# Paged decode attention: keys turned by VectorE in 32x32 blocks, block-diagonal queries

## What is computed

```python
def stick_breaking_weights(z, mask):
    log_keep = jnp.where(mask, jax.nn.log_sigmoid(-z), 0.0)
    remain = lax.cumsum(log_keep, axis=z.ndim - 1, reverse=True)
    return jnp.exp(jnp.where(mask, z + remain, -jnp.inf))

def sb_decode(q, k_new, v_new, k_past, v_past, bias):
    z_past = jnp.einsum('bqhd,bkhd->bhqk', q, k_past)
    z_new = jnp.einsum('bqhd,bkhd->bhqk', q, k_new)
    z = jnp.concatenate([z_past, z_new], axis=-1) * scale + bias[None, :, None, None]
    a = stick_breaking_weights(z, mask)          # mask: all of the past, causal in the new tokens
    return (jnp.einsum('bhqk,bkhd->bqhd', a[..., :P], v_past)
            + jnp.einsum('bhqk,bkhd->bqhd', a[..., P:], v_new))
```

## Time and profile before

| | us |
|---|---|
| timed runs, median of 3 | 1451.14 |
| lowest and highest | 1446.97, 1455.94 |
| span of the profiled execution | 1442.7 |
| PE busy in it | 1288.7 (89%) |
| VectorE busy | 400.6 (28%) |
| ScalarE busy | 353.6 (25%) |
| DMA, mean over the span | 274 GB/s |

### The profile page before, as it was taken

How to read it: one execution, slowest core, us unless ns; L and a number is a source line. 1 busy time by engine, 2 the same in 40 slices (tenths; PEclk the granted TensorE clock), 3 DMA queues, 4 the chain that set the end, 5 groups by cost and what they waited for, 6 DMA issues and landing times.

```text
span 1442.7 us, 22498 instructions
## 1 busy us (share of the span) xinstructions
PE 1288.7 (89%) x8892; PEld 778.3 (54%) x8892; DVE 400.6 (28%) x745; ACT 353.6 (25%) x575; POOL 87.3 (6%) x146
## 2 busy tenths in 40 slices
PE   7999999989999999878999999789987888788782
PEld 4787555756777666546888865533332333333231
DVE  2012565634544445431101123511111001101103
ACT  2122344444554445642000011200000000000000
POOL 3000000020000002000000000011101000100000
PEclk9999999999999989999999999889999889999887
DMA  6113301068999989999911150299999999999985
GB/s 237 59 59 117 111 1 61 27 182 302 386 375 381 379 303 386 385 386 348 392 35 37 59 235 31 88 367 427 424 425 426 425 426 426 426 425 426 427 367 198
DMA packets 119641, 395.96 MB, mean 274 GB/s; under 512 B 17075, under 2 KB 25284, under 8 KB 107250
## 3 DMA queue, kind: packets, MB, share of 16 engines
q1 hardware_dynamic: 109506, 380.41, 67.7%
q0 software_dynamic: 5984, 11.18, 2.2%
q10 hardware_dynamic: 4048, 2.93, 0.6%
HBM read 386.06 MB, written 16.27 MB: 279 GB/s over the span
## 4 chain that ended last, share of the span: by engine, by line
PE 79%; issue 7%; SPq 7%; DMA 4%; DVE 2%; ACT 1%; POOLq 0%; DVEq 0%
PE ps L1180 17%; PE ps L1002 8%; PE ps L694 8%; PE ps L1203 7%; PE ps L824 5%; PE ps L697 5%; PE ps L1005 4%; PE ps L1067 4%; SPq L411 3%; PE ps L858 3%; SPq L399 3%; PE ps L835 3%; DMA arena<-in_w_in 2%; DMA arena<-in_cache_k 1%; PE ps L1191 1%
## 5 line engine op out<-in xcount | busy, mean ns | idle before, releaser
L1180 PE MATMUL ps<-arena 128*64 128x512 f32 x512 | 253.8, 654 | 69.3 <-issue 67.8
L1181 PE MATMUL ps<-arena 128*64 128x512 f32 x512 | 254.3, 655 | 0.0
L1180 PEld LDWEIGHTS ps<-arena 128*64 128x64 f32 x512 | 74.2, 151 | 215.0 <-issue 212.9
L824 PE MATMUL ps<-ident,arena 128*128 128x128 f32 x1024 | 142.8, 283 | 25.4 <-DMA arena<-in_cache_k 24.9
L824 PEld LDWEIGHTS ps<-ident,arena 128*128 128x128 f32 x1024 | 112.3, 143 | 91.3 <-issue 59.3
L1410 ACT ACTIVATE arena<-ps 128x512 f32<-128x512 f32 x192 | 108.2, 596 | 162.7 <-PE ps L824 162.5
L1002 PE MATMUL ps<-mixers,arena 128*128 128x272 f32 x512 | 121.6, 399 | 4.9 <-DMA arena<-in_w_in 4.9
L694 PE MATMUL ps<-mixers,arena 128*128 128x272 f32 x512 | 119.3, 393 | 0.0
L1002 PEld LDWEIGHTS ps<-mixers,arena 128*128 128x128 f32 x512 | 98.8, 194 | 25.9 <-DMA arena<-in_w_in 5.1
L694 PEld LDWEIGHTS ps<-mixers,arena 128*128 128x128 f32 x512 | 96.7, 190 | 20.3 <-issue 0.4
L1821 DVE COPY arena<-ps 128x512 f32<-128x512 f32 x64 | 44.2, 691 | 163.9 <-PE ps L824 163.9
(11 more groups left out here) (343 smaller groups left out, 1393.2 us busy)
## 6 DMA issues: line engine op xcount, KB each, us to landing
arena<-in_cache_k SPq DMA_DIRECT2D x256, 256.0 KB, 5.6
arena<-in_w_gate_exp SPq DMA_DIRECT2D x32, 2048.0 KB, 32.4
arena<-in_w_up_exp SPq DMA_DIRECT2D x32, 2048.0 KB, 36.9
arena<-in_cache_v SPq DMA_DIRECT2D x252, 256.0 KB, 5.9
arena<-in_w_down_exp SPq DMA_DIRECT2D x22, 2048.0 KB, 37.6
mixers<-in_w_down_exp SPq DMA_DIRECT2D x10, 2048.0 KB, 37.7
arena<-in_w_in SPq DMA_DIRECT2D x7, 2048.0 KB, 9.4
arena<-in_w_in SPq DMA_DIRECT2D x8, 1024.0 KB, 15.6
```

The lines of the kernel that those rows point to most:

```text
L824: last = turn(ps[:, turned_at(n, j), P * c:P * c + P], keys_of(n)[:, j, P * c:P * c + P], ident[:, :])
L1180: mm(ps[0:BLK, 1 + u, :], own, wgv[w][:, k, :], start=k == 0, stop=k == KD - 1)
L1181: last = mm(ps[BLK:P, 1 + u, :], own, wuv[w][:, k, :], start=k == 0, stop=k == KD - 1)
```

## The change

**Keys.** PE no longer turns pages. VectorE turns a unit's four pages in one instruction, in blocks of 32x32 (`keys_turned`): input 128 x 2048 floats, output 128 x 2048, SBUF to SBUF. After it, partition 32g + k holds dimension k of a 32-wide slice of a head, for the tokens 32g to 32g + 31 of each page. The scores are therefore products with block-diagonal queries: 16 products of 128 columns in place of 4 of 512, with the queries of one sequence set out by four quarters of the tokens (`query_rows`, `query_blocks`, `in_g`).

**Sets.** A set is now four units of one sequence. A row of the score tile is a head pair, a quarter g of every page, and a query; the sum over the past needs what the other three quarters add. Two small products per set (`other_losses`) with two constant matrices, made by GpSimd in place of masks no longer used, bring it, and VectorE subtracts it in one more 128x512 instruction (`remains`).

**Values.** The turned weights have token 32g + r of page j at partition 4r + j. So the values are loaded in that order: page j goes to the 32 partitions j, j + 4, ..., and each of them receives four rows of the page, 2 KB each and 32 rows apart. The products have 8 rows instead of 32. A unit's four value loads stay 256 KB each.

```diff
@@ loads @@
-                b, g = PER_SET * (m // NGRP) + s, m % NGRP
-                first_page = b * NPAGES + NPAGES - GP * (g + 1)
+                b, later = m // SETS_OF, SETS_OF - 1 - m % SETS_OF
+                first_page = b * NPAGES + GP * (PER_SET * later + s)
             def key_loads(n):
                 if n >= 3:
-                    sp.wait_ge(S("page_turned"), GP * (n - 2))
+                    sp.wait_ge(S("keys_turned"), n - 2)
             def value_loads(n):
                 for j, page in enumerate(numbers):
-                    sp.dma_start(values_of(n)[:, j, :], a["cache_v"][0, bass.ds(page, 1)].rearrange("a s h d -> (a s) (h d)")
-                                 ).then_inc(S(values_signal(n)[0]), 16)
+                    sp.dma_start(values_of(n)[j::GP], a["cache_v"][0, bass.ds(page, 1)].rearrange(
+                        "a (g s) h d -> (a s) g (h d)", g=4)).then_inc(S(values_signal(n)[0]), 16)
@@ PE @@
-            def turn_pages(n, pair):
...
+                pe.wait_ge(S("keys_turned"), n + 1)
-                for c in range(CT):
-                    last = mm(ps[32 * c:32 * c + 32, ZB, :], qblk_of(m // NGRP, s, c), d_kt[:, n % 2, c, :],
-                              start=s == 0, stop=s == PER_SET - 1)
+                for x in range(4):
+                    for c in range(CT):
+                        last = mm(ps[32 * c:32 * c + 32, ZB, P * s:P * s + P], wq[:, m // SETS_OF % 2, 4 * c + x, :],
+                                  d_kt[:, n % 2, 4 * c + x, :], start=x == 0, stop=x == 3)
+            def other_losses(m):
+                pe.wait_ge(S("set_ends"), m + 1)
+                mm(ps[:, bank, 0:16], neg_lt, own[:, 0:16], start=True, stop=False)
+                mm(ps[:, bank, 0:16], tri_ge, own[:, 1:17], start=False, stop=True).then_inc(S("other_losses"), 1)
@@ unit_values @@
-                        last = mm(ps[32 * c:32 * c + 32, VB, P * s:P * s + P], d_at[:, m % 2, j, 32 * c:32 * c + 32],
-                                  values_of(n)[:, j, P * c:P * c + P], start=m % NGRP == 0 and s == 0 and j == 0,
+                        own = d_at[:, m % 2, s, 32 * c + 8 * g:32 * c + 8 * g + 8]
+                        last = mm(ps[32 * c:32 * c + 8, VB, at:at + P], own,
+                                  values_of(n)[:, g, P * c:P * c + P], start=n % SEQ_UNITS == 0 and g == 0,
@@ VectorE @@
-                    v.tensor_copy(d_kt[:, n % 2, :, P * j:P * j + P], each(ps[:, turned_at(n, j), :], CT)).then_inc(S("kT_dve"), 1)
+            def keys_turned(n):
+                dve.wait_ge(S(f"cache_k_{n % 3}"), (n // 3 + 1) * 16 * GP)
+                if n >= 2:
+                    dve.wait_ge(S("unit_scores"), n - 1)
+                out = d_kt[:, n % 2].rearrange("p b (j k) -> p j b k", j=GP)
+                v.transpose(out, keys_of(n).rearrange("p j (b k) -> p j b k", k=32)).then_inc(S("keys_turned"), 1)
+            def remains(m):
+                dve.wait_ge(S("other_losses"), m + 1)
+                v.tensor_tensor(each(d_z, 16), each(d_z, 16), ps[:, others_at(m), 0:16].unsqueeze(2).to_broadcast([P, 16, 32]),
+                                ALU.subtract).then_inc(S("set_sums"), 1)
@@ ScalarE @@
-            def keys_out(n, pages=range(GP - 1)):
-                    fn(d_kt[:, n % 2, :, P * j:P * j + P], each(ps[:, turned_at(n, j), :], CT), ACT.Copy).then_inc(S("kT_act"), 1)
+                fn(d_e.rearrange("p (u k j) -> p u j k", u=PER_SET, j=GP), d_z.rearrange("p (u j k) -> p u j k", u=PER_SET, j=GP),
+                   ACT.Exp).then_inc(S("set_weights"), 1)
```

More of the change, by code:

```diff
@@ L786, in _ @@
                     attn_values(h // 2 - 1)
+                if h == H - 1:
+                    pe.wait_ge(S("attn_out"), CT - 1)
+                    for x in range(4):
+                        for g in range(4):
+                            last = mm(ps[32 * g:32 * g + 32, 3, P * x:P * x + P], ident[:, 32 * x:32 * x + 32],
+                                      qT[:, :, SEQ:T], start=True, stop=True)
+                    last.then_inc(S("query_rows"), 1)
                 attn_remain(h)
@@ L792, in new_scores @@
                 for c in range(CT):
-                    own = qblk_of(0, 0, c)
-                    own = bass.AP(own.tensor, own.offset,
-                                  [list(own.ap[0]), [PER_SET * CT * 32, NSET], [CT * 32 + 8, PER_SET], [1, 8]])
-                    last = mm(ps[0:TS, 4, 64 * c:64 * c + 64], kT[:, c, SEQ:T], own, start=True, stop=True)
+                    for e in range(2):
+                        hs = slice(64 * e, 64 * e + 64)
+                        last = mm(ps[0:TS, 4 + e, TS * c:TS * c + TS], kT[hs, c, SEQ:T], qT[hs, c, SEQ:T], start=True, stop=True)
                 last.then_inc(S("new_products"), 1)
@@ L802, in new_sums @@
                 mm(ps[:, 7, 0:1], brow[0:1, :], ones[0:1, 0:1], start=True, stop=True)
-                for sg in range(NSET):
-                    for c in range(CT):
-                        own = n_L[0:TS, 64 * c + 32 * sg:64 * c + 32 * sg + 32]
-                        last = mm(ps[32 * c:32 * c + 32, 7, 1 + sg:2 + sg], own, ones[0:TS, 0:1], start=True, stop=True)
+                for c in range(CT):
+                    last = mm(ps[32 * c:32 * c + 32, 7, 1:1 + NB], new_g[0:TS, 32 * c:32 * c + 32], in_b[:, :],
+                              start=True, stop=True)
                 last.then_inc(S("new_products"), 1)
@@ L1823, in losses @@
             def losses(m):
+                own = d_ends[:, m % 2]
                 dve.wait_ge(S("set_softplus"), 4 * m + 3)
                 rounding(d_e, d_t)
+                if m >= 2:
+                    dve.wait_ge(S("other_losses"), m - 1)
+                if m:
+                    dve.wait_ge(S("set_ends"), m)
+                before = d_ends[:, (m - 1) % 2, 0:1] if m % SETS_OF else d_c[:, 1 + m // SETS_OF:2 + m // SETS_OF]
+                chain(v.tensor_copy(own[:, 16:17], before))
@@ L1835, in losses @@
-                dve.wait_ge(S("set_sums"), 2 * m + 1)
-                v.tensor_tensor(d_z, d_z, d_R, ALU.subtract).then_inc(S("set_sums"), 1)
+                chain(v.tensor_tensor_scan(out=d_R[:, ::-1], data0=d_t[:, ::-1], data1=d_ln[:, ::-1],
+                                           initial=own[:, 16:17], op0=ALU.add, op1=ALU.add))
+                chain.wait()
+                v.tensor_copy(own[:, 0:16], each(d_R, 16)[:, :, 0]).then_inc(S("set_ends"), 1)
+                chain(v.tensor_tensor(d_z, d_z, d_R, ALU.subtract))
@@ L1869, in _ @@
                     losses(m - 1)
+                if m and s == 1:
+                    remains(m - 1)
                 if n == PER_SET * NGRP + LAG - 1:
```

176 lines of the change are left out of this document (96 added, 80 removed).

## The result

The changed kernel takes 1518.6 us (median of 4 runs, 1515.9 to 1523.0), the kernel before, on the same chips, 1449.1 us (4 runs, 1443.8 to 1455.9). The ratio is 1.048, with a 95% interval of 1.044 to 1.052: slower by 70 us. The forecast was 1572 with a range of 1434 to 1600. The sign and the range held, the size was too large by 53 us, and the reason given was for the most part not the reason, as the experiments show.

A forecast was written before the change was run, and what follows sets the result against it. The prediction took DMA to bound decode nearly everywhere, PE close behind. From a 1442.7 us span, +126 for value loads, -12 for PE and +7 at the end gave 1564, then 1572 as timed; range 1434 to 1600.

The forecast's parts named there:

- rival C: Decode: the block transpose takes two passes, VectorE becomes the bound, +58 us, 1509; chance 0.06.
- the 7 us at the tail: After the gate weights: six units of values at the slower load rate, with the last unit's products, add 7 us.
- I take the row it is nearest to, 0.55: Decode value loads: 0.55 of 385 GB/s, as the y_sample store into 32 partitions suggests; 2.21 us a unit, +126 us.
- Rival B: Decode: the new value loads lose nothing, DMA binds at 385 GB/s, -12 us, 1439; chance 0.30.
- the rival of a half loss: Decode value loads: engines meet only half of the time, 63 us lost, less 12, 1502; chance 0.10.
- Nothing counted: Decode: PE and VectorE wait for each other's sums once a set, 22 us if shown, covered by keys two units ahead.
- Rival D: Decode: the wait for VectorE's sums shows in full, 22 us, at a full value rate, 1461; chance 0.04.
- PE's relief: Decode: less PE work gives back what PE took from the DMA rate, 12 us saved.
- the -6 to +6 that the prediction had for the start: Kernel's start: added instructions against small copies gone, counted as 0 us, with -6 to +6.
- Share about 1, rate 270 to 280, values landing well above keys, PE under half busy: Decode: signs that would show the forecast of slow value loads right, rate in GB/s.
- the main theory: Decode: value loads into 32 partitions lose their rate in full, giving 1572; chance 0.50.
- VectorE waiting for L867: Decode: with a DMA share clearly below 1, the sign that the wait for sums shows, 1461.

The follow-up runs named there:

- e3: Changed kernel with PE doing the scores of unit n - 1 in place of unit n: 1486.1 us, ratio 1.025.
- e1: Kernel before with only the changed value loads, 32 partitions four apart, four rows of 2 KB into each: 1478.2 us, ratio 1.020.
- e7: Kernel before with each value load into 32 neighbouring partitions, four rows each: 1665.5 and 1678.0 us, ratio 1.150.
- e8: Kernel before with value loads into partitions four apart, one piece of 8 KB each: 1459.1 us, ratio 1.003.
- e11: Kernel before with all four pages of unit n turned, then the scores of that same unit: 1501.2 us, ratio 1.034.
- e9: Changed kernel with VectorE's `remains`, the set's weights and their turning each one unit later: 1497.1 us, ratio 1.031.
- e2: Changed kernel with the value loads of before, a page row to a partition: 1511.0 us, ratio 1.041.
- e5: Changed kernel with scores one unit later and the value loads of before: 1447.2 us against 1453.1, ratio 0.996.

## Why the prediction was right and wrong

**Right, in good part by luck.** The change makes the kernel slower, and the time is inside the stated range. But the term that made the forecast slow is worth 8 to 42 us, by the run, and not 126, and the largest cause stood nowhere in the sum; e3, without that cause, takes 1486. The block transpose takes 2.300 us (forecast 2.3, from the row of L1809), and two passes (rival C) are out. A unit's score products take 1.08 us at the full clock, and 1.94 at the lower one. VectorE fits: busy 273 of 434 us. The stages from the gates on stay as they were, within 6 us (785.8 against 780.4), so the 7 us at the tail can be neither shown nor excluded.

**Wrong: "I take the row it is nearest to, 0.55".** This term carried +126 us. Alone it measures +27 (e1). The step that failed is the choice of y_sample's row for the new loads. The prediction said itself that the new partitions are four apart and y_sample's are neighbours, and then let the count of 32 decide. The runs with the count held at 32 cost 219, 27 and 6 us (e7, e1, e8), so the count is not what decides. With neighbours the engines are held, as the row said (1256 us of packets in place of 977). Four apart they are not (997 and 975 in e1 and e8, 995 in e11 with the old loads); the step left out what SyncE needs to issue a load, 602 ns in place of 332, which makes 5.87 us a unit against 5.45 of transfers. That this is the whole of the 27 us is not shown.

By the Trainium skill, SBUF — State Buffer, section Door 1, neighbours reach half of the ports and partitions four apart all of them. The packets' times of e1 and e8 agree with the second half, e7's with the direction of the first, though 0.38, if the keys kept their rate, is below the half that counting ports gives. Rival B (no loss) missed the form's cost by those 27 us, the rival of a half loss (63 us) was too high as well. The prediction's own range of 1540 to 1600 was also summed too high at its lower end: at 0.65 of 385 a unit's values take 4.19 us, 57 x 1.47 = 84 us more, which makes some 1525.

**Wrong: "Nothing counted" for the new wait, and cover by the buffers.** The prediction saw that PE waits for VectorE and VectorE for L867, priced it at 22 us, and called it covered, since keys are two units (10.9 us) ahead. A buffer that is ahead covers late data. It doesn't cover a loop in which PE waits for VectorE's transpose of this unit and VectorE for PE's products that stand behind this unit's scores: in such a unit their pieces follow one another, however early the keys are. VectorE never waits for the scores themselves. It waits once a set for L867 (40 us in decode), and at mixer steps for PE's L923, L957 and L945 (20.5, 15.9 and 4.5 us); of such waits at mixer steps the kernel before has none and e3 4 us. e9 takes the one wait for L867 away and gives 22 us back. Its size was short too: at most 1.4 us a set, said the prediction; of the 56.0 us in 16 waits for L867 one is 16.2, after decode under the gate products, and the other fifteen are 2.65 us each.

**Missed: the lost distance of one unit.** This is the largest single cause: 32 us alone (e3), 64 us with the loads of before (e2 to e5), and 49 us in the kernel before (e11). The part on PE counted 16 transposes gone and 2.2 us a unit left, and never looked at where the scores stood: formerly a unit behind the turning, now right behind it. The order of instructions had shown it, and no term of the sum asked about it. Rival D was of this kind, but had only the wait for the sums, at 1461.

**PE's relief: 12 us forecast, 6 measured.** e5 has the relief, the loads of before and the unit's distance, and gives 1453.1 - 1447.2 = 5.9 us (interval 3 to 9). From 350 to 500 us it reaches 383 GB/s instead of 375, as forecast; the rest is lost at the start, where 300 to 350 us run at 249 GB/s in e5 against 282 in the kernel before. The 1.65 MB that this leaves (50 us times 33 GB/s) are 4.3 us at 385 GB/s, inside the -6 to +6 that the prediction had for the start.

**The signs to look for.** "Share about 1, rate 270 to 280, values landing well above keys, PE under half busy": the share was 0.88, the rate 298, values 4.3 us against 4.2 for keys, PE 65% busy. Each of the four spoke against the main theory at the first look. "VectorE waiting for L867" was there, as the sign of D.

**The sum again, from measured terms.** From 1.041 - 0.996 for the order on its own (64 us), 0.029 for the form once the stream of loads is the bound (39 to 42 us) and -6 for PE's relief one would come to nearly 100; 70 were measured, since the two losses overlap. The reading that fits is that a unit takes the longer of the loop and the loads, and that both show only where they are close.

**Open.** Whether SyncE's issue is all of the form's cost: no run gives the new loads a faster issue or the old ones a slower one. Why a load with partitions four apart takes 602 ns to issue in short pieces and 472 in long ones, and one with neighbours 316. How keys and values share the slow stream of e7. And the fallen clock's part in the loop. No version here that computes all of the reference beats the kernel before: e5 is 6 us faster, but with values in their old places, which don't fit its weights.

## What to carry to other kernels

When work moves from one engine to another, write down for both engines how many steps lie between the one that makes a piece and the one that uses it, before and after. With a distance of zero, and a wait the other way as well, the pieces of both follow one another, and full buffers of input don't help; the marks are a DMA share below 1, no engine full, and two engines in each other's waits. And price a load in a new form twice: by the transfer, for which it matters where its partitions lie and not how many there are, and by what the issuing engine needs for one unit's loads, which must stay below the time of their transfers. A time to landing that falls together with the rate is the mark of a slow issue.

## What the runs showed of the hardware

- Streams with value loads of 256 KB into 32 partitions beside key loads into 128, at 350 to 500 us: neighbours 213 GB/s in all at a share of 1.06 (e7), four apart in pieces of 2 KB 336 at 0.97 (e1), four apart in pieces of 8 KB 359 at 0.99 (e8), all into 128 partitions 375 at 1.03.
- The shortest issue on SyncE of a load of 256 KB: 128 partitions of 2 KB 332 ns (before), 32 neighbours 316 (e7), 32 four apart in pieces of 8 KB 472 (e8), in pieces of 2 KB 602 (e1).
- A VectorE transpose in 32x32 blocks, f32, of 128x2048 takes 2300 ns, of 128x1024 1239 ns: 1.04 ns for an element more.
- A shorter time to landing is not a faster stream: in e1 values land in 4.3 us where they took 5.9, at 345 GB/s instead of 385.
- The granted clock was 0.98 over decode with PE busy 328 of 361 us, and 0.70 with PE busy 284 of 434; the same 32 score instructions took 1.08 us at the one level and 1.94 at the other.
